# Two causal attentions on one core: values summed two parts behind the turning instead of one, with four buffers of turned tiles instead of three

## The reference

```python
# FoX: causal per frame, a decay bias from a cumulative sum
s = einsum('bqhd,bkhd->bhqk', qb, k) * scale + (cq[..., :, None] - cum[..., None, :])
s = where(kpos[None, :] <= qpos[:, None], s, -inf)
out = einsum('bhqk,bkhd->bqhd', softmax(s), v)
# DSA: one shared k and v; only the 256 keys that an indexer scores highest
_, sel = lax.top_k(iscore, topk)
s = where(valid, einsum('bqhd,bqkd->bhqk', qb, k[sel]) * scale, -inf)
out = einsum('bhqk,bqkd->bqhd', softmax(s), v[sel])
```

## Time and profile before

| | |
|---|---|
| median of three runs | 2728.52 us |
| profiled execution, its span | 2745.2 us (first to last instruction; no time around it is given) |
| mean granted TensorE clock | 0.942 of full |
| PE busy | 2549.6 us, 93% of the span |
| DVE / ACT / POOL busy | 1247.2 / 1081.5 / 365.6 us |
| `fox`, first to last matmul | 410.6 to 581.9 us |
| `dsa`, first to last matmul | 589.1 to 726.3 us |

### The profile page before, as it was taken

One profiled execution on the slowest core, in us unless ns is written; L12 is line 12 of the kernel. 1 busy time (PEld: TensorE's weight loads), 2 busy tenths in 40 slices (PEclk: granted clock), 3 DMA queues, 4 the chain that ended last, 5 costly groups with the idle time before them and its releaser, 6 DMA issues. The chain is left out here.

```text
span 2745.2 us, 30591 instructions
## 1 busy us (share of the span) xinstructions
PE 2549.6 (93%) x12099; PEld 2130.3 (78%) x12099; DVE 1247.2 (45%) x2002; ACT 1081.5 (39%) x1601; POOL 365.6 (13%) x188
## 2 busy tenths in 40 slices
PE   4889878989799999999999979996999999999998
PEld 3668657889688888888887767895878888888877
DVE  4464666665443333333336634543433333324365
ACT  4344776656533222222225533443322222223254
POOL 1111103301011222222000011000112222220000
PEclk8999989999999999999999989756999999999999
DMA  4101100000231111111336621004311111113375
GB/s 126 38 21 42 31 16 24 24 1 1 74 126 55 53 47 46 54 46 46 123 94 215 205 62 31 1 1 102 106 54 48 53 47 46 54 46 115 100 238 176
DMA packets 163465, 191.42 MB, mean 70 GB/s; under 512 B 11284, under 2 KB 132468, under 8 KB 163324
## 3 DMA queue, kind: packets, MB, share of 16 engines
q1 hardware_dynamic: 158016, 171.46, 20.3%
q10 hardware_dynamic: 5308, 18.01, 1.7%
HBM read 172.64 MB, written 16.81 MB: 69 GB/s over the span
## 5 line engine op out<-in xcount | busy, mean ns | idle before, releaser
L128 PE MATMUL l_ps<-rest_hi,l_whi 128*128 128x512 f32 x1408 | 440.6, 390 | 4.7 <-DVE rest_lo L1891 4.7
L128 PE MATMUL l_ps<-rest_hi,l_wlo 128*128 128x512 f32 x1408 | 439.8, 390 | 0.0
L128 PE MATMUL l_ps<-rest_lo,l_whi 128*128 128x512 f32 x1408 | 439.8, 390 | 0.0
L1758 POOL TENSOR_TENSOR l_wlo<-l_raw,l_whi 128x1024 fp32r<-128x1024 f32 x88 | 213.1, 2422 | 985.2 <-ACT l_whi L1677 985.2
L128 PEld LDWEIGHTS l_ps<-rest_hi,l_whi 128*128 128x128 f32 x1408 | 265.1, 188 | 60.2 <-DVE rest_lo L1891 5.2
L128 PEld LDWEIGHTS l_ps<-rest_hi,l_wlo 128*128 128x128 f32 x1408 | 265.1, 188 | 55.2
L128 PEld LDWEIGHTS l_ps<-rest_lo,l_whi 128*128 128x128 f32 x1408 | 265.2, 188 | 54.9
L1677 ACT ACTIVATE l_whi<-l_raw 128x1024 fp32r<-128x1024 f32 x156 | 164.2, 1052 | 127.2 <-PE l_ps L128 119.1
L1897 DVE SCALAR_TENSOR_TENSOR l_y_v<-l_ps,main_conv,l_y_v 128x1023 f32<-128x1023 f32 x44 | 56.4, 1283 | 337.7 <-ACT l_y_v L1711 337.7
L1711 ACT ACTIVATE l_y_g<-l_ps,main_conv 128x1024 f32<-128x1024 f32 x44 | 53.1, 1207 | 383.9 <-PE l_ps L128 383.9
L1897 DVE SCALAR_TENSOR_TENSOR l_y_g<-l_ps,main_conv,l_y_g 128x1023 f32<-128x1023 f32 x44 | 56.5, 1283 | 284.5 <-ACT l_y_g L1711 284.5
(11 more groups left out here) (319 smaller groups left out, 4796.3 us busy)
## 6 DMA issues: line engine op xcount, KB each, us to landing
l_raw<-in_ffn_w_in SPq DMA_DIRECT2D x88, 512.0 KB, 4.0
l_raw<-in_ffn_w_out SPq DMA_DIRECT2D x68, 512.0 KB, 3.7
l_rawl<-in_ffn_w_out SPq DMA_DIRECT2D x44, 512.0 KB, 4.0
front_raw<-in_even_w_in SPq DMA_DIRECT2D x20, 512.0 KB, 3.6
l_rawe<-in_ffn_w_out SPq DMA_DIRECT2D x20, 512.0 KB, 3.7
odd_raw<-in_odd_w_qkv SPq DMA_DIRECT2D x10, 512.0 KB, 4.0
setup_xin<-in_x SPq DMA_DIRECT2D x8, 512.0 KB, 10.9
fox_negc<-negc_dram SPq DMA_DIRECT2D x8, 512.0 KB, 3.7
```

What stands on the lines that cost most here:

```text
L128: mm = pe.matmul(o, w, m, start=a, stop=z)
L1758: pool.tensor_tensor(wlo[u % 3][:], raw_up[u % 2][:], whi[u % 3][:].bitcast(F32), ALU.subtract).then_inc(up_lo, 1)
```

## The change

`values` moves from one part behind `turn` to two, on PE in both stages. `probT` gets four slots instead of three (2 KB more per partition), and `copy` waits for the slot's user of four parts before. The three banks `TR` stay. DVE's `normalise` moves one part later with the `values` that it waits for, and DVE's loop has one round more.

```diff
     RING, AHEAD, EXP_AHEAD, NP, ROWS, GRP = 3, 5, 3, 6, 8, 4
+    BEHIND, PT = 2, 4
...
-        pT = st.sb("probT", [P, RING, HALF])
+        pT = st.sb("probT", [P, PT, HALF])
...
-                        mm = pe.matmul(O[grp % 2][:, i * VW:(i + 1) * VW], pT[:, j % RING, k - c:k - c + P], steps[n]["v"](k // P),
+                        mm = pe.matmul(O[grp % 2][:, i * VW:(i + 1) * VW], pT[:, j % PT, k - c:k - c + P], steps[n]["v"](k // P),
...
-                for j in range(NPARTS + 1):
+                for j in range(NPARTS + BEHIND):
                     if j + AHEAD < NPARTS:
                         scores(j + AHEAD)
                     if j < NPARTS:
                         turn(j)
-                    if j >= 1:
-                        values(j - 1)
+                    if j >= BEHIND:
+                        values(j - BEHIND)
...
-                    if j >= RING:
-                        act.wait_ge(summed, j - RING + 1)
-                    act.activation(pT[:, j % RING, 0:e - c], TR[j % RING][:, 0:e - c], ACT.Copy).then_inc(copied_act, 1)
+                    if j >= PT:
+                        act.wait_ge(summed, j - PT + 1)
+                    act.activation(pT[:, j % PT, 0:e - c], TR[j % RING][:, 0:e - c], ACT.Copy).then_inc(copied_act, 1)
...
-                for j in range(NPARTS + AHEAD + 2):
+                for j in range(NPARTS + AHEAD + BEHIND + 1):
...
-                    while groups < N // GRP and last[groups * GRP + GRP - 1] + AHEAD + 1 <= j:
+                    while groups < N // GRP and last[groups * GRP + GRP - 1] + AHEAD + BEHIND <= j:
```

More of the change, by code:

```diff
@@ L1384, in copy @@
                     dve.wait_ge(T_ready, j + 1)
-                    if j >= RING:
-                        dve.wait_ge(summed, j - RING + 1)
-                    dve.tensor_copy(pT[:, j % RING, 0:e - c], TR[j % RING][:, 0:e - c]).then_inc(copied_dve, 1)
+                    if j >= PT:
+                        dve.wait_ge(summed, j - PT + 1)
+                    dve.tensor_copy(pT[:, j % PT, 0:e - c], TR[j % RING][:, 0:e - c]).then_inc(copied_dve, 1)
                 def normalise(grp):
```

## The result

The changed kernel takes 2708.05 us (median of 8 runs, 2700.88 to 2721.41), the kernel before 2730.09 us (8 runs). The ratio is 0.9931, interval 0.9915 to 0.9947: faster by 0.5 to 0.85%. The medians differ by 22.0 us; the forecast was 2706 us, 22.7 us less. The range held the time. The runs scatter by up to 0.5% of their median, and the profiled executions show scatter of that size outside the two stages: from the start of the turning stage to the end they took between 1990 us (mean clock 0.97) and 2018 us (0.95), with no code changed there. `fox` repeats to 0.2 us in kernels whose `fox` is the same, and `dsa` to 0.5 us with one part behind and 1.4 us with more, so the experiments are read by these stages first.

A forecast was written before the change was run, and what follows sets the result against it. PE was taken to bound `dsa` by its own work, `fox` also losing 14.9 us idle and 11.6 to the clock. Gains of 11.0 + 2.0 + 9.7 = 22.7 us off 2728.5 gave 2706 us, range 2701 to 2719.

The forecast's parts named there:

- The six packings and the 1.30 us before the third: `fox`: PE's waits of `values` for the `copy` behind each packing, plus one before the third; 11.0 of 12.7 us go.
- The walk: Second packing in `fox`, timed from part 6's turning: 1.91 us more PE work before part 8's `values`, against waits of 1.68 to 2.06.
- what is left is at most 0.15 us at a packing: `fox`: PE's remaining wait behind a packing once the added work fills it; some 0.4 us over all of them.
- the moved `normalise`: DVE: `normalise` a part later, at most 2.8 us more per head, hidden in 5.6 us of waits for `scores`; cost 0.
- The other waits and `dsa`: Three short waits in `fox` (2.1 us) and two in `dsa` (0.8), `values` behind a late `copy`; 2.0 us gained.
- The clock: 9.7 us expected: `fox`: five of six clock falls behind the packing waits go, 9.7 of the 11.6 us lost to the lower clock.
- signs named beforehand: Expected in the profile after, among others: `fox` waits for `copy` fall from 14.8 to 1 to 3 us; `dsa` changes under 1.
- The clock falls all the same: Rival, 0.16: `fox` waits go but the clock still falls around packings; only 13 us gained, 2715.5 us.
- DVE becomes the bound: Rival, 0.09: in `fox` DVE holds up `scores` in bursts; 7.9 us gained, 2720.6 us.
- The place of the wait only moves: Rival, 0.07: PE's wait moves to `turn` for `exp` or to the next `copy`; no change, 2728 us.
- The clock stays low: Rival, 0.04: `fox` stays at clock 0.50 though PE is busy; 100 us of it would give 2765.5 us.

## Why the prediction was right, and where it was off

*The six packings and the 1.30 us before the third: 11.0 us expected.* The seven waits were 12.7 us and are 5.1 (0.78, 0.25, 1.83, 0.25, under 0.15, 1.95): 7.6 us gone. The walk was exact at the second packing, and I used it for all six. It holds while DVE is in time; the step that failed is "what is left is at most 0.15 us at a packing". The rest at the third was expected (1.45, measured 1.83), those at the first and the sixth were not. Both the spread packing and the earlier chores take the sixth away: it needs the late `exp` and the block together. Another step failed with it: the moved `normalise` was put at cost 0, since DVE has idle time enough over the stage. What counts is where it stands: 0.56 us ahead of the `bias_max` that the last `exp` needs, which is most of the first packing's 0.78.

*The other waits and `dsa`: 2.0 us expected.* In `fox`, 0.99, 0.83 and 0.29 are gone; 0.57, 0.28 and twice 0.15 us are there instead: 1.0. In `dsa` it is 3.7, after the lower clock at its start. I took that wait from PE's row (0.8), where the weight load's row, 3.4, is much the nearer. In `fox` PEld's waits fell by 9.5 us and PE's by 8.9.

*The clock: 9.7 us expected,* 11.6 - 1.7 = 9.9 measured. Five of six falls went, as I had assumed, but the one that stayed is at the sixth packing (1.95 us), not at the third (1.83).

*Sum:* 22.7 expected; 7.6 + 1.0 + 3.7 + 9.9 = 22.2 by the parts, 23.3 in the stages, 22.0 in the medians. The closeness is partly luck: 3.4 us too much at the packings and 2.7 too little for the other waits and `dsa` nearly cancel. Two of the signs named beforehand missed by the same errors: the waits for the copies in `fox` came to 5.9 us (1 to 3 forecast), and `dsa` changed by 3.7 (less than 1 forecast).

*The rivals.* "The clock falls all the same" is excluded for this kernel (0.99). "DVE becomes the bound" is not so for PE directly (0.3 us of `scores` waits), but in part by way of ACT: its waits for DVE rose from 10.5 to 23.0 us and make what is left. "The place of the wait only moves" is wrong at two and begins to show at three parts behind (1.1 us). "The clock stays low" did not happen here, but did with the packing doubled.

## What to carry to other kernels

Where PE consumes what another engine copies, and that engine has a block of other work now and then, count what PE still has between its last step that is ready and the one that waits, against the block: one part more in between (here 1.9 us of PE work at that place) takes up to that much of the wait away and needed no further buffer here. Look too at what else moves with the order, as the `normalise` did. Cut the block as well: spreading ACT's 3.2 us over three parts took 16.0 us off `fox`, the distance 19.6, both 26.0. A wait of 2 us can cost about twice its length where the clock falls behind it; and a wait for a stationary operand is read from the weight load's rows as well as from the matmul's.

## What the runs showed of the hardware

The clock's reaction is no simple function of one wait: in the changed kernel 1.83 us (466.43) leave it at 1.00 and 1.95 us (522.20) bring it down, and in the kernel with the packing spread and one part behind 1.99 us (499.19) do not, where a wait of 1.30 us (465.01) was followed by its one fall, as its rows show:

```profile
462.00:474.00 12.00, 10.54 (x70) 9.58 (x70) 6.66 (x22) 9.18 (x15) 4.64 (x2) 0.86 0.13 45
...
495.00:506.00 11.00, 9.01 (x73) 8.30 (x71) 9.16 (x25) 6.24 (x10) 2.00 (x1) 1.00 0.11 46
```

The very same wait can go either way. In the kernel before, the 1.68 us at the fifth packing (517.45) are followed by the low level (0.74 from 518 to 530 us) and by no further wait before the sixth. With only the slot added the same 1.68 us (517.10) leave the clock at 1.00, and the fall comes behind a wait of 1.51 us (526.16) that the kernel before does not show; `fox` takes 178.5 and 178.7 us. The rows of the second:

```profile
512.00:525.00 13.00, 10.97 (x87) 9.92 (x85) 9.49 (x18) 8.68 (x15) 7.55 (x3) 1.00 0.11 40
525.00:534.00 9.00, 7.84 (x48) 7.39 (x49) 7.09 (x20) 4.77 (x8) 0.00 (x0) 0.81 0.01 3
```

With waits of 3.1 to 4.9 us (packing doubled, two behind) every 22 to 29 us it was 0.81 over `fox`, with 4.8 to 5.2 us (one behind) 0.87: the shorter waits had the lower clock.
